# TensorE takes the products of each mixing step at the step's own place in the order, not behind the next projection unit

## What is computed

```
for each layer:
  n = rmsnorm(h);  u = n @ w_in                  # 25 blocks of 128 columns: gates, ax, ag, q, k, bv, ci, cf, ...
  A: causal conv of ax, two gates, linear recurrence (RG-LRU)       width 256
  B: sliding-window attention, window 128, rotary, sinks            4 q heads, 2 kv heads
  C: HGRN2, a gated linear recurrence with 64x64 states             4 heads
  D: mLSTM, a 64x64 matrix memory with a max stabiliser             4 heads
  h += concat(A, B, C, D) @ w_out
  h += relu(rmsnorm(h) @ w_up)^2 @ w_down        # d_ff 4096
  h += sigmoid(h @ w_gate) * (p @ w_proj)        # "ple"
returns h and the states of A to D, for the prompt and for the samples
```

## Time and profile before

| | us |
|---|---|
| median of 3 executions | 3361.98 (3361.32 to 3364.65) |
| the profiled execution | 3366.12 |
| its span, first to last instruction | 3364.3 |
| TensorE (PE) busy | 2975.5, 88% |
| VectorE (DVE), GpSimd (POOL), ScalarE (ACT) busy | 1369.8, 1408.3, 1157.7 |
| mean granted clock of TensorE | 0.93 |

### The profile page before, as it was taken

The page is one execution under the profiler, slowest core; times in us unless marked ns, Lnnn a source line. Parts: engine busy times, 40 slices in busy tenths (PEclk is TensorE's granted clock), DMA queues, the critical chain, the costliest instruction groups (busy, mean ns, idle before and its releaser), DMA issues.

```text
span 3364.3 us, 43826 instructions
## 1 busy us (share of the span) xinstructions
PE 2975.5 (88%) x18104; PEld 2575.0 (77%) x18104; DVE 1369.8 (41%) x2373; ACT 1157.7 (34%) x1763; POOL 1408.3 (42%) x880
## 2 busy tenths in 40 slices
PE   4677787979999898898989889787999989999998
PEld 3456577767787687788987788775878867899998
DVE  4444235436533464334452336443655242222222
ACT  4423254323332344433223234442333233422232
POOL 1143143326643463334543255332564337445454
PEclk8777788989999998899999999898999999999999
DMA  2111022223222242222222124222322223323232
GB/s 93 44 38 32 25 92 66 72 81 94 76 77 63 84 138 70 69 64 70 75 68 78 45 79 142 63 77 69 94 77 74 72 65 121 106 89 94 88 100 83
DMA packets 80293, 261.26 MB, mean 78 GB/s; under 512 B 10722, under 2 KB 12002, under 8 KB 80096
## 3 DMA queue, kind: packets, MB, share of 16 engines
q1 hardware_dynamic: 63008, 228.04, 21.9%
q10 hardware_dynamic: 17088, 30.43, 2.6%
HBM read 244.90 MB, written 13.54 MB: 77 GB/s over the span
## 4 chain that ended last, share of the span: by engine, by line
PE 72%; DVE 13%; ACT 5%; POOL 4%; issue 3%; DMA 2%; ACTq 0%; SPq 0%; DVEq 0%
PE pj L474 21%; PE pj L476 20%; PE pj L475 20%; DVE sl L1465 3%; POOL w_lo L1342 2%; PE pm L557 2%; DMA sl<-in_vc 2%; PE pm L731 2%; DVE att L1855 1%; ACT w_hi L886 1%; PE pm L828 1%; PE pm L833 1%; DVE hid L1465 1%; DVE sl L1611 1%; POOL m_lo L1433 1%
## 5 line engine op out<-in xcount | busy, mean ns | idle before, releaser
L1342 POOL TENSOR_TENSOR w_lo<-w_raw,w_hi 128x1024 fp32r<-128x1024 f32 x428 | 1042.1, 2439 | 1517.3 <-ACT w_hi L886 1517.2
L474 PE MATMUL pj<-hid,w_hi 128*128 128x260 f32 (+1 forms) x1920 | 643.0, 335 | 96.2 <-DVE hid L1465 34.5
L474 PE MATMUL pj<-m_hi,w_hi 128*128 128x260 f32 (+1 forms) x1920 | 627.9, 327 | 31.5 <-POOL w_lo L1342 14.1
L476 PE MATMUL pj<-hid,w_lo 128*128 128x260 f32 (+1 forms) x1920 | 627.6, 327 | 0.0
L476 PE MATMUL pj<-m_hi,w_lo 128*128 128x260 f32 (+1 forms) x1920 | 619.1, 322 | 0.0
L475 PE MATMUL pj<-m_lo,w_hi 128*128 128x260 f32 (+1 forms) x1920 | 618.5, 322 | 0.0
L886 ACT ACTIVATE w_hi<-w_raw 128x1024 fp32r<-128x1024 f32 x428 | 446.6, 1051 | 371.5 <-PE pj L476 338.1
L475 PE MATMUL pj<-hid,w_hi 128*128 128x260 f32 (+1 forms) x1536 | 501.7, 327 | 0.0
L474 PEld LDWEIGHTS pj<-hid,w_hi 128*128 128x128 f32 x1920 | 373.6, 195 | 145.5 <-DVE hid L1465 41.0
L474 PE MATMUL pj<-n_hi,w_hi 128*128 128x260 f32 (+1 forms) x1200 | 405.5, 338 | 75.5 <-DVE n_lo L1506 29.4
L474 PEld LDWEIGHTS pj<-m_hi,w_hi 128*128 128x128 f32 x1920 | 366.6, 191 | 68.6 <-POOL w_lo L1342 17.6
(11 more groups left out here) (303 smaller groups left out, 3336.5 us busy)
## 6 DMA issues: line engine op xcount, KB each, us to landing
w_raw<-in_w SPq DMA_DIRECT2D x428, 512.0 KB, 3.5
out_y<-res ACTq DMA_DIRECT2D x16, 260.0 KB, 4.7
out_y<-res ACTq DMA_DIRECT2D x16, 256.0 KB, 4.7
sl<-in_x ACTq DMA_DIRECT2D x4, 520.0 KB, 5.4
res<-in_x ACTq DMA_DIRECT2D x8, 260.0 KB, 4.6
res<-out_y ACTq DMA_DIRECT2D x8, 260.0 KB, 4.8
res<-in_x SPq DMA_DIRECT2D x4, 512.0 KB, 6.7
res<-out_y ACTq DMA_DIRECT2D x8, 256.0 KB, 5.3
```

The lines of the kernel that those rows point to most:

```text
L474: pe.matmul(out, wh, hi[:, k, c0:c1], start=(k == 0), stop=False)
L476: last = pe.matmul(out, wl, hi[:, k, c0:c1], start=False, stop=(k == n - 1))
L1342: pool.tensor_tensor(w_lo[:, j % RAW_BUFS, :], w_raw[:, j % RAW_BUFS, :], w_hi[:, j % HI_BUFS, :].bitcast(F32), ALU.subtract).then_inc(lo_ ...
```

## The change

The place of the mixing steps in TensorE's list: the held steps now stand ahead of the dense step that ends the holding, not behind its first part. D0, S1, S2, D1 of `ORDER` is now D0, S1, S2, D1 on TensorE too. Nothing else differs; the rows of ACT, DVE, POOL and of the DMA queue stay as they are, and TensorE's 15995 rows are the same ones in another order.

```diff
--- before.py
+++ after.py
@@ -230,7 +230,7 @@
             continue
         halves = x[0] == 'ple' and x[1] % 2 or x[0] == 'down' and (x[3] or x[1] % 2)
         parts = [(x, p) for p in range(2 if halves else 1)]
-        out += parts[:1] + held + parts[1:]
+        out += held + parts
         held = []
     return out + held
 
```

## The result

The changed kernel takes **3382.19 us** (median of 4, 3380.40 to 3383.63) against 3361.65 for the kernel before (median of 4): ratio 1.0061, 95% interval 1.0048 to 1.0073. It is slower by 0.6%, or 20 us. I had forecast 17 us less, 3345, in a range up to 3385. Its profiled execution has a span of 3381.8 us, 17.5 more than before.

A forecast was written before the change was run, and what follows sets the result against it. TensorE bounds the kernel, so only its 389 us of standing still and its clock could change. Pass 0, the two odd passes and pass 2 gave 5 + 13 + 13 - 48 = -17 us: 3345, range 3318 to 3385.

The forecast's parts named there:

- Pass 2, -48: Mixing of pass 2: most eviction stalls go (-46), lost covers cost +10, recovered clock gives -12; -48 us.
- Passes 1 and 3, "+13 each": Mixing of the odd passes: lost covers and clock outweigh small gains; +13 us each, bounds 0 and +25.
- (a): Ahead of the first sattn: gate and rope lose cover, mostly taken out of the 16.6 us transfer wait; +1 us.
- (b): At sattn 2: needs the end of a long DVE chain with one unit less in front; +5.7 us.
- (c): At hdiag: loses the unit that covered POOL's making of its operand; +5.1 us.
- (d): At hsamp 2: waits for DVE's chain over the sample states; +3 us.
- (e): At the HGRN chunks: 4.5 of the 8.0 us of hid waits go; -4.5 us.
- (i): Clock in each odd pass: a quarter of the 13 us of waits that (b) to (d) add, guessed; +3 us.
- Pass 0, +5: Mixing of pass 0: gate 0 costs +0.4 and hdiag +4.6; +5 us, bounds -5 and +12.
- A: Covers lost whole: +37 us per odd pass, +11 in pass 0, -35 in pass 2; 3412 us, 22 in 100.
- B: No net change: DVE's step still precedes evictions, so half of pass 2's stalls stay; 3362 us, 15 in 100.
- C: Odd passes lose nothing (+3 us each), pass 0 gives 0, pass 2 gives -64; 3304 us, 13 in 100.

The follow-up runs named there:

- `own_pass2`: Against the kernel before: mixing steps at their own place on TensorE in pass 2 alone, one unit later elsewhere as before; 3317.96 us, ratio 0.9877.
- `split_b`: Against the kernel before: own place for all pass 2, pass 0's rope, rot, vt, attn, pass 1's sattn, pass 3's hprep, hdiag, hsamp; 3345.20 us.

## Why the prediction was wrong

*What bounds the kernel.* Right for pass 2: the stalls of the earlier trace rows came from TensorE's own lateness by way of DVE's order, and went when it went (`own_pass2`).

*Pass 2, -48.* Measured -50.8. The terms: idle -46 + 10 = -36 against -32.2, clock -12 against -18.6. That the sum fits within 3 us is partly luck: the idle time was overrated by 4 and the clock underrated by 7.

*Passes 1 and 3, "+13 each": this is the term that failed*, with +31.9 and +27.3. By its parts:
- (a), what is lost ahead of `sattn` "is taken out of" the wait for the transfer, +1. This was wrong in kind, not in size. The transfer's end was not at a time of its own: its issue is chained to attention's last products, and the loss ahead of it moved it. I had read its landing and not what releases its issue. Gate and rope brought +3.4 (no more than chance can give) and attention +5.7 in the runs that split them. With (b), the changed kernel lost 18.0 and 13.5 us up to the end of `sattn`, where I had put 6.7.
- (b), `sattn` 2, +5.7: the mechanism was right, but together with `sattn` 0 it measured +11.7.
- (c) and (d), `hdiag` and `hsamp`, 5.1 + 3 = 8.1: measured +16.0 in `split_b`. The waits were 4.3 and 3.1 us, sized nearly right; what lay on top is for the most part the clock (6.4).
- (e), -4.5 from the chunks: the `hid` waits of 8.0 did go, but in the run that moved hE, hP and hnorm alone the stretch grew by 1.9, and there they only fell to 4.3 while line 731 (of the kernel before), a product of `hP`, waited 4.7 us anew. What was won at the projections was lost at the mixing steps. With (c) and (d) that makes 14.7 and 13.8 us in the changed kernel, where I had put 3.6.
- (i), +3 for the clock, "a guess from a quarter" of the waits: measured +11.6 and +7.8. In the odd passes the clock took four to nine tenths of the new standing still, not a quarter: 11.6 us beside 20.3 in pass 1, 7.8 beside 19.5 in pass 3, 6.4 beside 7.4 at `hdiag` and `hsamp`. And I had counted only the waits that (b) to (d) add.

*Pass 0, +5.* The standing still grew by 5.0; the clock, which I had put at nothing, took 6.2 more. Where in the pass is only partly settled: the front alone gave -1.4 and -1.6, the HGRN part alone +6.9, and the sum of these is 7 us short of the +11.3 of all of it.

*The sum.* Idle time: forecast -11, measured +12.6. Clock: forecast -6, measured +7.0. Of the miss of 37 us the idle time of the odd passes is 20, their clock 13, the clock of pass 0 6, and pass 2 took 3 off it.

*The rivals.* A named the right mechanism for the odd passes (covers lost whole, +37 each against +30 measured on average) and a wrong size for pass 2 (-35 against -51), so its 3412 was 30 us off where my 3345 was 37 off, on the other side. I had given it 22 in 100. The evidence for it stood in my own rows: in the earlier trace rows the gate begins at the moment at which its operand is ready, and in the earlier trace rows `hdiag` begins 1.1 us after POOL was done with `att` (757.04 is where POOL went on to `ex`), so the unit in front was nearly their whole cover. B (evictions stay late behind DVE's own step) and C (nothing lost in odd passes) are both out.

## What to carry to other kernels

A delay between producer and consumer engines is neither good nor bad by itself: it is worth the work that it hides, and it is free as long as the buffers behind the late engine hold more units than the delay; count buffers in units of the stretch at hand (three banks were three `up` units in one pass and one and a half in the next), and set the delay per stretch. When a step loses its cover, price the wait at more than its length if TensorE's clock falls behind it: in the odd passes here it was 1.4 to 1.9 times. And before calling a transfer's landing fixed, look up what releases its issue.

## What the hardware showed unexpectedly

Filling a wait of 4.3 us with 18 products that nobody reads made the stretch behind it faster: clock 0.85 in place of 0.66, 3.7 us of 16 back for two waits. Small products are hit as well: eight of 128x2 took 1.84 us in place of 0.95 behind the wait.
